# Two attention output projections: finer head waits, and the last two weight slabs interleaved by column half

## What is computed

```python
# mla_mixer (head outputs o: 256 x 1024)
outs.append(jnp.einsum('bhqk,bkhd->bqhd', p, v[:, :end]))
o = jnp.concatenate(outs, axis=1).reshape(bsz, seq, N_HEADS * V_HEAD_DIM)
return o @ w_o
# moba_mixer, here with a single block of 256 keys
p = jax.nn.softmax(s_own, axis=-1).astype(v_own.dtype)
return jnp.einsum('hqk,hkd->hqd', p, v_own)
...
return o @ w_o
# around each: x = x + mixer(rmsnorm(x, gain)); then h = rmsnorm(x, ...) for the next block
```

## Time and profile before

| | us |
|---|---|
| median of 3 runs | 2160.53 (2159.04 to 2161.24) |
| profiled execution | 2165.21 |
| its span, first to last instruction | 2163.5 |
| TensorE busy | 2106.7, 97% |
| DVE busy | 1422.5, 66% |
| ACT busy | 1183.7, 55% |
| DMA | 457 MB, 211 GB/s mean |
| granted TensorE clock, mean | 0.991 |

### The profile page before, as it was taken

How to read it: one execution, slowest core, us unless ns; L and a number is a source line. 1 busy time by engine, 2 the same in 40 slices (tenths; PEclk the granted TensorE clock), 3 DMA queues, 4 the chain that set the end, 5 groups by cost and what they waited for, 6 DMA issues and landing times.

```text
span 2163.5 us, 28129 instructions
## 1 busy us (share of the span) xinstructions
PE 2106.7 (97%) x10448; PEld 1763.6 (82%) x10448; DVE 1422.5 (66%) x1483; ACT 1183.7 (55%) x1362; POOL 56.2 (3%) x102
## 2 busy tenths in 40 slices
PE   9999999899999999998999999999999999989999
PEld 8888887678878878877888777888788899878887
DVE  5654556479898988998454675545544588575444
ACT  4454456476877777776444565444444466554443
POOL 1000001000000000000100010000000000000000
PEclk9999999999999999999999999999999999989999
DMA  7555443179898898998455443555454445214551
GB/s 286 185 182 187 167 159 117 70 275 359 345 346 336 342 366 322 356 351 330 160 189 188 159 159 141 189 184 185 174 188 167 163 148 207 104 59 175 191 184 52
DMA packets 64296, 457.09 MB, mean 211 GB/s; under 512 B 7328, under 2 KB 7664, under 8 KB 9552
## 3 DMA queue, kind: packets, MB, share of 16 engines
q1 hardware_dynamic: 63616, 455.24, 57.1%
q0 software_dynamic: 448, 0.46, 0.2%
q10 hardware_dynamic: 144, 0.20, 0.0%
HBM read 454.82 MB, written 1.05 MB: 211 GB/s over the span
## 4 chain that ended last, share of the span: by engine, by line
issue 63%; PE 30%; DVE 3%; ACT 1%; DVEq 1%; POOL 1%; DMA 0%; POOLq 0%; ACTq 0%; SPq 0%
PE gu L1902 4%; PE gu L1904 4%; PE gu L1903 4%; PE acc L1902 3%; PE acc L1904 3%; PE acc L1903 3%; PE acc L1980 2%; PE acc L1982 2%; PE acc L1981 2%; DVE wlo L1151 1%; PE tp L1994 0%; DVEq L1726 0%; ACT whi L640 0%; POOL qk_rstd L610 0%; DMA raw<-in_slabs 0%
## 5 line engine op out<-in xcount | busy, mean ns | idle before, releaser
L1151 DVE TENSOR_TENSOR wlo<-raw,whi 128x2048 fp32r<-128x2048 f32 (+1 forms) x436 | 989.0, 2272 | 425.1 <-ACT whi L640 424.0
L640 ACT ACTIVATE whi<-raw 128x2048 fp32r<-128x2048 f32 (+1 forms) x436 | 827.4, 1898 | 237.1 <-PE acc L1904 190.4
L1902 PE MATMUL gu<-whi,actA_hi 128*128 128x512 f32 (+1 forms) x1456 | 579.2, 398 | 2.9 <-DVE actA_lo L1163 1.8
L1904 PE MATMUL gu<-whi,actA_lo 128*128 128x512 f32 (+1 forms) x1456 | 568.2, 390 | 0.0
L1903 PE MATMUL gu<-wlo,actA_hi 128*128 128x512 f32 (+1 forms) x1456 | 567.1, 390 | 0.0
L1902 PEld LDWEIGHTS gu<-whi,actA_hi 128*128 128x128 f32 x1456 | 274.2, 188 | 59.5 <-issue 3.9
L1904 PEld LDWEIGHTS gu<-whi,actA_lo 128*128 128x128 f32 x1456 | 274.0, 188 | 58.2
L1903 PEld LDWEIGHTS gu<-wlo,actA_hi 128*128 128x128 f32 x1456 | 274.8, 189 | 53.0
L1902 PE MATMUL acc<-whi,hT_hi 128*128 128x512 f32 x656 | 256.4, 391 | 5.0 <-DVE wlo L1151 2.8
L1904 PE MATMUL acc<-whi,hT_lo 128*128 128x512 f32 x656 | 255.7, 390 | 0.0
L1903 PE MATMUL acc<-wlo,hT_hi 128*128 128x512 f32 x656 | 255.4, 389 | 0.0
(11 more groups left out here) (400 smaller groups left out, 2179.0 us busy)
## 6 DMA issues: line engine op xcount, KB each, us to landing
raw<-in_slabs SPq DMA_DIRECT2D x427, 1024.0 KB, 4.8
raw<-in_slabs SPq DMA_DIRECT2D x4, 576.0 KB, 3.7
raw<-in_slabs SPq DMA_DIRECT2D x2, 768.0 KB, 4.1
raw<-in_slabs SPq DMA_DIRECT2D x2, 640.0 KB, 3.8
x<-in_x SPq DMA_DIRECT2D x2, 512.0 KB, 4.3
out<-x SPq DMA_DIRECT2D x2, 512.0 KB, 2.8
vecs<-in_vecs ACTq DMA_DIRECT2D x1, 192.0 KB, 4.1
raw<-in_slabs SPq DMA_DIRECT2D x1, 128.0 KB, 3.0
```

Source lines behind the costliest of these rows:

```text
L640: act.activation(whi[:, n0 % SPLIT, 0:w], raw[:, n0 % RAW, 0:w], ACT.Copy).then_inc(slab_hi, 1)
L1151: dve.tensor_tensor(wlo[:, n0 % SPLIT, 0:w], raw[:, n0 % RAW, 0:w], whi[:, n0 % SPLIT, 0:w].bitcast(F32), ALU.subtract).then_inc(slab_spli ...
L1902: pe.matmul(o, xh, wh, start=start, stop=False)
L1904: return pe.matmul(o, xl, wh, start=False, stop=stop)
```

## The change

In MLA, `out_part` becomes one k block of one half, and the order of the last two slabs is written out: slab 12 half 0 (both blocks), then, with a wait for seven heads, slab 13's first block of half 0, then slab 12's half 1, then, with the wait for eight heads, slab 13's second block of half 0, the first of half 1, the transposes of the next norm and the second of half 1. The positions run on as before, 88 to 103. The split of slab 14 stands at position 98 in place of 92, behind the last head's values_hi and values_lo. In MoBA slab 12 waits for two heads and slab 13 for four.

```diff
--- before.py
+++ after.py
@@ -393,7 +393,7 @@
             return gu[:, t] if c == 0 else acc[:, 2 * ((c + 1) % 2) + t]
 
         ML_AT = [0, 8, 16, 24, 32, 40, 46, 52, 60, 66, 72, 80, 88, 96]
-        ML_SPLIT = (4, 12, 17, 28, 33, 38, 48, 56, 64, 70, 76, 84, 92, 100)
+        ML_SPLIT = (4, 12, 17, 28, 33, 38, 48, 56, 64, 70, 76, 84, 98, 100)
         ML_T = (54, 58, 62, 66, 71, 75, 79, 83)
         ML_R = (53, 60, 71, 77)
         ML_V = (65, 69, 73, 77, 82, 86, 90, 94)
@@ -2208,39 +2208,52 @@
                                 r.then_inc(slab_used, 1)
                             head_steps(ML_AT[n] + 2 * kt + t)
 
-                def out_part(n, half):
+                def out_part(n, half, j, g):
                     sl = (f.s0 + n) % SPLIT
                     w = [z[:, sl].rearrange("p (k n) -> p k n", k=2) for z in (whi, wlo)]
                     ns = slice(512 * half, 512 * half + 512)
-                    for j in range(2):
-                        kt = 2 * (n - 10) + j
-                        for t in range(NT):
-                            ts = slice(t * P, (t + 1) * P)
-                            r = three(acc[:, 2 * half + t], actB_hi[:, kt, ts], actB_lo[:, kt, ts], w[0][:, j, ns], w[1][:, j, ns],
-                                      kt == 0, kt == 7)
-                            if j and t:
-                                if half:
-                                    r.then_inc(slab_used, 1)
-                                elif n == 13:
-                                    r.then_inc(ml_half, 1)
-                            head_steps(ML_AT[n] + 4 * half + 2 * j + t)
-                            if n == 13 and half and j == 0 and t == 1:
-                                norm_early(f.after)
-
-                for n in range(14):
+                    kt = 2 * (n - 10) + j
+                    for t in range(NT):
+                        ts = slice(t * P, (t + 1) * P)
+                        r = three(acc[:, 2 * half + t], actB_hi[:, kt, ts], actB_lo[:, kt, ts], w[0][:, j, ns], w[1][:, j, ns],
+                                  kt == 0, kt == 7)
+                        if t:
+                            if half and j:
+                                r.then_inc(slab_used, 1)
+                            elif n == 13 and j:
+                                r.then_inc(ml_half, 1)
+                        head_steps(g + t)
+
+                for n in range(10):
                     wait_slab(f.s0, n)
                     if n < 4:
                         down(n)
                     elif n in (4, 7):
                         keys_values(n)
-                    elif n < 10:
+                    else:
                         queries(n)
-                    else:
-                        pe.wait_ge(ml_olo, 2 * (n - 9))
-                        for half in range(2):
-                            if n == 10:
-                                pe.wait_ge(ml_evac, 7 + half)
-                            out_part(n, half)
+                for n in (10, 11):
+                    wait_slab(f.s0, n)
+                    pe.wait_ge(ml_olo, 2 * (n - 9))
+                    for half in range(2):
+                        if n == 10:
+                            pe.wait_ge(ml_evac, 7 + half)
+                        for j in range(2):
+                            out_part(n, half, j, ML_AT[n] + 4 * half + 2 * j)
+                wait_slab(f.s0, 12)
+                pe.wait_ge(ml_olo, 6)
+                out_part(12, 0, 0, 88)
+                out_part(12, 0, 1, 90)
+                wait_slab(f.s0, 13)
+                pe.wait_ge(ml_olo, 7)
+                out_part(13, 0, 0, 92)
+                out_part(12, 1, 0, 94)
+                out_part(12, 1, 1, 96)
+                pe.wait_ge(ml_olo, 8)
+                out_part(13, 0, 1, 98)
+                out_part(13, 1, 0, 100)
+                norm_early(f.after)
+                out_part(13, 1, 1, 102)
 
             def moba(f):
 
@@ -2343,8 +2356,8 @@
                     projected(n)
                 for n in (12, 13):
                     wait_slab(f.s0, n)
+                    pe.wait_ge(mb_olo, 2 * (n - 11))
                     if n == 12:
-                        pe.wait_ge(mb_olo, 4)
                         pe.wait_ge(mb_evac, 5)
                     out_part(n, 1, True)
                     if n == 12:
```

## The result

The changed kernel took **2164.99 us** (median of 20 runs, 2161.75 to 2168.46); the kernel before, run between them, took 2162.23 (20 runs, 2157.25 to 2166.25). The ratio is **1.0013, 95% interval 1.0007 to 1.0019**. So it is slower by about 2.8 us: within the 0.2% that were called no change, but its interval leaves out zero, and the time lies above the range of 2158.7 to 2163.7.

A forecast was written before the change was run, and what follows sets the result against it. TensorE was taken to bound the kernel, busy 2106.7 of 2163.5 us. MoBA -1.47, MLA +1.48 and clock +0.8 summed to +0.8 on 2160.53, giving 2161.3 us, range 2158.7 to 2163.7.

The forecast's parts named there:

- MoBA: Second attention: slab 12's first output group waits for two heads, so head 7's transposes come 1.47 us earlier; bounds 0 and 2.15.
- MLA: First attention: add_half(0) queues on DVE behind both later splits, so the next norm's transposes come 1.48 us later.
- The clock: Behind MLA's new idle gap of about 3.4 us the clock falls to half, costing +0.8 us; bounds 0 and 1.6.
- Rival (d): Clock stays down over the whole serial router stretch after MLA: up to 5.4 us, 2165.9; chance 0.06.
- The base: Whole kernel: the sum was set on 2160.53 us, the median of the runs shown, 4.7 below the profiled time.
- (a): The clock stays up behind MLA's new gap: +0.0, 2160.5 us; chance 0.25.
- (b): MLA gain kept: both splits done before add_half is wanted, transposes at 402.6; -1.9 and -1.47 give 2157.2; chance 0.10.
- (c): MoBA's group really waited for the split the list names, nothing gained there: +1.48 + 0.8, 2162.8 us; chance 0.07.

The follow-up runs named there:

- inter_split92: The changed kernel with slab 14's split put back at position 92, so interleaving alone in MLA, MoBA part kept; 2163.47 us, ratio 1.001.
- after: The changed kernel itself, both parts in, against the kernel before; here its first profiled execution; median 2164.99 us, ratio 1.0013.
- before_again: The kernel before, unchanged, run and profiled once more in another set; 2162.35 us, ratio 1.0.
- both_fixed_late: As both_fixed, but DVE's split of slab 15 stands behind the routing's last step (choose_pair) instead of ahead of it; 2157.51 us, ratio 0.9979.
- mla_fixed: The changed kernel with ACT splitting slab 14 at 92, DVE's part behind values_lo(7), and DVE's split of slab 15 moved into the router; 2160.21 us, ratio 0.9996.
- both_fixed: As mla_fixed, and in MoBA DVE's split of slab 13 moved from 94 to 95, behind values_lo of head 3; 2159.54 us, ratio 0.9989.

## Why the prediction was right and wrong

**MoBA (right).** -1.47 was forecast, -1.44 measured: the first output group had waited for four heads and not for the split that the list of waits named, and the wait moved to the next transposes (about 0.7 forecast, 0.81 measured). Alone it gave -1.0 at equal clock.

**MLA (right).** Counted from position 88, forecast and measured: group 92 at +4.00 and +3.96, values_lo(7) at 7.43 and 7.38, the first split on DVE at 9.22 and 9.26, add_half(0) at 13.62 and 13.67, the transposes at 15.05 and 15.10, the gap 3.4 and 3.39. The loss of 1.48 came as +1.53. What I hadn't seen is that the loss has two sufficient causes; I had put it all to the order of the splits, and inter_split92 missed for it. No cost of SP's later reloads is seen: the rest at equal clock is +0.1 over 32 runs, and the two distances ask for +0.09.

**The clock (the failed step).** I wrote "Bounds 0 and 1.6; I take the middle, +0.8". The fall itself came, and in its own place it cost 0.7 to 1.0, within these bounds. But the kernel as a whole ran at a mean clock lower by 0.0015, worth +2.4 (0.4) by the line through the runs. The step's error is that I priced one fall, in one place, and took that for the bound. The kernel has other places where the clock is down in some executions and not in others: a second fall, at the router's end, cost another 1.6 (25.1 us to the experts for 23.5) in those executions that had it. A price of the clock has to be taken over them all, and its upper bound was not 1.6. Where the whole +2.4 arises stays open: the fall behind the gap explains 1.0 to 1.3 of it, and the profiles are too few for the rest. Rival (d) named a larger price, but by one long low stretch over the router, and that is not what happened: in after the clock was back at 1.00 from 412 on, and where it fell again, it did so some 14 us later.
The Trainium skill, TensorE: Matmul & The Clock Gate, section HAM oscillation, says that long idle gaps between bursts of matmuls bring the half rate back, each time one comes. For the gaps of 2.70 to 3.40 us ahead of T1 the traces agree, 8 times in 8. For the shorter gap of 2.15 us in MoBA they do so in some executions only: 1.00 in the earlier trace rows, 0.50 in before_again, and a fall in two of the six executions that have this gap.

**The base.** 2160.53 was the median of three runs of a kernel whose 122 runs average 2162.12 with a deviation of 2.2. The three were 1.6 low. I had set the sum on that median, and widened the range by the spread of the same three, 2.2, where the runs of this kernel spread from 2157 to 2167. The range does not follow from its own terms either: 2160.53 with +1.48 for MLA, nothing for MoBA and 1.6 for the clock is already 2163.6, so the 2163.7 holds next to none of the 2.2 us that were to be added. Of the 3.7 us between 2161.3 and 2164.99, some 1.6 to 1.7 are the base, about 1.6 the clock (+2.4 against +0.8), and the remainder is within the error. The chances (0.94 for within 0.2%) fitted; the range didn't, for these reasons.

**Rivals.** (a) is out, the clock fell behind the gap each time. (b) and (c) are out, by T1 and by MoBA's distance. Of (b)'s reading something remained: with the order of both_fixed_late its gain and more is there, and it is not the interleaving but the second split in front of add_half(0) that stood in the way.

## What to carry to other kernels

Before a wait is shortened by moving a long instruction behind it, follow that instruction to the next thing queued behind it on its own engine: here most of the 2.2 us of waits in front of TensorE went, and came back as 1.5 lost and a gap of 3.4; moving the second split out of the way brought the transposes 1.7 us ahead of the kernel before. A gap that brings the clock down can cost more than the low stretch behind it shows (here 1.0 there, 2.4 in the mean of 32 runs), so price it over the mean clock of many runs. Products that nobody reads, in the gap, kept the clock up there, but a fall came 7 us later instead; only with the second thin place filled as well was the loss gone. Where a kernel's runs spread by 2 us, neither three runs nor one profiled execution are a base for tenths; distances between marks in the trace are.

## What the runs showed of the hardware

- A POOL instruction on 128x2 elements took 1.05 us beside DVE's 128x2048 split in mla_fixed and both_fixed, and 0.19 in the kernel before and in both_fixed_late; it ended 0.06 and 0.05 us after the split. The Trainium skill, SBUF — State Buffer, section Who interferes with whom, says that DVE and GpSimd share a pair of ports under an exclusive lock, and the trace agrees: the one that started later ended only when the first was through.
- The places where the clock is down recur from execution to execution, but which of them are taken, and for how long, varies within one kernel: the end of the router in one profiled execution and not in the next, 3 or 10 us some 630 us after position 88. The line through the runs takes a standard deviation of some 2 us within a kernel down to 0.9, so this is the larger part of why runs differ.
- A fall of the clock cost 0.7 to 1.0 us behind T1, 1.6 in the router and, in before_again, 1.2 in MoBA's gap, each by the distance between two marks.
- A wait for more than one semaphore can carry the wrong name: MoBA's 2.15 us stood against the split L1151, and went away when the wait for two more heads did.
